# Combining a group of experts in threes behind the next group's gate/up slots

## What is computed

```python
# 4 groups x 8 experts = 32 experts, top 2 of one group for each token
def expert_block(args):
    rt, rg, e = args
    xb = x_pad[rt]
    hb = jax.nn.silu(xb @ w_gate[e]) * (xb @ w_up[e])      # 2048 -> 512
    return (hb @ w_down[e]) * rg[:, None]                  # 512 -> 2048
...
return jax.ops.segment_sum(out.reshape(P, D), row_tok, num_segments=T + 1)[:T]
```

## Time and profile before

| | |
|---|---|
| median of 3 runs | 1612.42 us (1610.18 to 1615.23) |
| span of the profiled execution | 1613.5 us |
| TensorE (PE) busy | 1272.8 us, 79% of the span |
| PE weight loads (PEld) busy | 655.1 us |
| VectorE busy | 393.7 us, 24% |
| ScalarE busy | 378.5 us, 23% |
| DMA | 475.38 MB, mean 295 GB/s over the span |
| mean granted TensorE clock | 0.896 |

### The profile page before, as it was taken

The page is one execution under the profiler, slowest core; times in us unless marked ns, Lnnn a source line. Parts: engine busy times, 40 slices in busy tenths (PEclk is TensorE's granted clock), DMA queues, the critical chain, the costliest instruction groups (busy, mean ns, idle before and its releaser), DMA issues.

```text
span 1613.5 us, 19649 instructions
## 1 busy us (share of the span) xinstructions
PE 1272.8 (79%) x7570; PEld 655.1 (41%) x7571; DVE 393.7 (24%) x737; ACT 378.5 (23%) x643; POOL 31.9 (2%) x41
## 2 busy tenths in 40 slices
PE   5999999999899996677677677568678666766765
PEld 4999998566566641221122122122122112212212
DVE  6354443245554330120120120120113012012013
ACT  5333322143433221112112112112120111211213
POOL 1001000001000000000000000000000000000000
PEclk9999999999899988888878889879897888988987
DMA  9444540123433389999989999999976998999993
GB/s 322 140 144 154 157 138 33 37 81 107 129 125 106 130 338 420 420 374 420 421 363 422 421 373 420 421 406 390 420 293 247 420 421 366 421 420 384 422 420 139
DMA packets 110801, 475.38 MB, mean 295 GB/s; under 512 B 14156, under 2 KB 51136, under 8 KB 60304
## 3 DMA queue, kind: packets, MB, share of 16 engines
q1 hardware_dynamic: 109776, 470.86, 73.3%
q0 software_dynamic: 832, 2.48, 0.4%
q10 hardware_dynamic: 64, 0.02, 0.0%
HBM read 469.96 MB, written 3.38 MB: 293 GB/s over the span
## 4 chain that ended last, share of the span: by engine, by line
PE 61%; DMA 26%; issue 7%; DVE 2%; ACT 1%; SPq 1%; ACTq 0%; DVEq 0%
DMA ring<-in_w_up 14%; PE ps L843 12%; DMA ring<-in_w_down 11%; PE ps L871 7%; PE ps L574 5%; PE ps L575 5%; PE ps L576 5%; PE ps L858 5%; PE ps L822 3%; PE ps L746 2%; PE ps L635 2%; PE ps L662 2%; PE ps L755 2%; PE ps L748 2%; PE ps L747 2%
## 5 line engine op out<-in xcount | busy, mean ns | idle before, releaser
L843 PE MATMUL ps<-ring,mix 128*32 128x512 f32 x2112 | 335.6, 772 | 242.9 <-issue 131.6
L843 PEld LDWEIGHTS ps<-ring,mix 128*32 128x32 f32 x2112 | 75.3, 131 | 495.7 <-issue 322.0
L1533 DVE TENSOR_TENSOR mix<-mix,ps 128x128 f32<-128x128 f32 x33 | 9.5, 288 | 765.5 <-ACT mix L1166 765.5
L1163 ACT COPY mix<-ps 128x512 f32<-128x512 f32 x33 | 35.5, 1076 | 616.0 <-PE ps L843 616.0
L574 PE MATMUL ps<-xT_hi,w_hi 128*128 128x320 f32 (+1 forms) x528 | 165.8, 314 | 3.9 <-DVE work L1258 3.9
L575 PE MATMUL ps<-xT_lo,w_hi 128*128 128x320 f32 (+1 forms) x528 | 164.8, 312 | 0.0
L576 PE MATMUL ps<-xT_hi,w_lo 128*128 128x320 f32 (+1 forms) x528 | 164.6, 312 | 0.0
L858 PE MATMUL ps<-ring,mix 128*32 128x512 f32 x1056 | 122.3, 596 | 29.4 <-DVE mix L1533 17.6
L871 PE MATMUL ps<-mix 128*128 128x512 f32 (+1 forms) x192 | 99.6, 678 | 23.9 <-ACT mix L1171 23.1
L822 PE MATMUL ps<-r,work 128*32 128x512 f32 (+1 forms) x816 | 107.9, 616 | 0.4 <-DVE work L1516 0.2
L1272 DVE TENSOR_TENSOR w_lo<-ring,w_hi 128x1024 fp32r<-128x1024 f32 (+1 forms) x66 | 76.8, 1205 | 117.3 <-ACT w_hi L978 117.3
(11 more groups left out here) (259 smaller groups left out, 1117.4 us busy)
## 6 DMA issues: line engine op xcount, KB each, us to landing
ring<-in_w_gate SPq DMA_DIRECT2D x128, 1024.0 KB, 20.7
ring<-in_w_up SPq DMA_DIRECT2D x128, 1024.0 KB, 22.8
ring<-in_w_down SPq DMA_DIRECT2D x128, 1024.0 KB, 23.6
ring<-in_w_in SPq DMA_DIRECT2D x32, 1024.0 KB, 8.1
ring<-in_w_o SPq DMA_DIRECT2D x16, 1024.0 KB, 6.2
hreg<-in_x_prompt SPq DMA_DIRECT2D x4, 1024.0 KB, 6.1
ring<-in_w_uq SPq DMA_DIRECT2D x4, 768.0 KB, 4.9
ring<-in_w_uv SPq DMA_DIRECT2D x2, 1024.0 KB, 5.9
```

What stands on the lines that cost most here:

```text
L843: last = pe.matmul(ps[r:r + B, 2, :], x[:, c + o, s, :], w[:, m, c + o, :], start=s == 0 and c == 0, stop=s == 3 and c == 2)
```

## The change

The 12 units of a group's combination leave the end of the iteration. They now stand in the next iteration, in threes behind `gate_up` of slots 0, 1, 2 and 3 of its first expert. Units 0 to 2 stand behind slot 0's matmuls, with the waits that stood before the whole combination. The first iteration has no group before it: it combines a `yg` and a `gT` that DVE sets to zero ahead of the loop. The last group is combined behind the loop, 12 units in a row. DVE's additions move likewise, to the head of the first expert of the next iteration. All counts of `comb_added`, `y_copied` and `gt_copied` shift by one group or one copy. Table row 2 now has the extra blocks before an expert, and a new row 4 those up to and with it.

The combination of an extra block gets a function of its own, with four banks, 4 to 7: bank `4 + n` for column block `n`. The four units of a token tile are issued together; those of the next tile wait for the addition of the same column block.

```diff
+            def combine_units(units, added_before):
+                for u in units:
                     i, n = u // 4, u % 4
                     t0, tn = TILES[i]
                     if u >= 3:
-                        pe.wait_ge(free_sem, value(u - 2))
-                    gates, rows = parts(n)
-                    pe.matmul(ps[0:tn, 5 + u % 3, :], gates[:, t0:t0 + tn], rows, ...).then_inc(full_sem, 1)
+                        pe.wait_ge(comb_added, added_before + (u - 2))
+                    pe.matmul(ps[0:tn, 5 + u % 3, :], gT[:, t0:t0 + tn], yg[:, 512 * n:512 * n + 512],
+                              start=True, stop=True).then_inc(comb_full, 1)
+
+            def combine_extra(x):
+                for i, (t0, tn) in enumerate(TILES):
+                    for n in range(4):
+                        if i:
+                            pe.wait_ge(x_added, x * 12 + (4 * (i - 1) + n + 1))
+                        rows = slice(B * n, B * (n + 1))
+                        pe.matmul(ps[0:tn, 4 + n, :], gTx[rows, t0:t0 + tn], yx[rows, :],
+                                  start=True, stop=True).then_inc(x_full, 1)
...
                     for s in range(4):
                         pe.wait_ge(slot_full[s], e * 32 + expert_count(s))
                         gate_up(xg, s).then_inc(weights_used, 1)
+                        if b == 0:
+                            if s == 0:
+                                pe.wait_ge(y_copied, q * 4 + 1)
+                                pe.wait_ge(gt_copied, q + 1)
+                                drained_extra = pe.value_load(tables[0:1, 2, bass.ds(q * 4, 1)], ...)
+                                pe.wait_ge(x_added, drained_extra)
+                                pe.wait_ge(comb_added, q * 12 + 1)
+                            combine_units(range(3 * s, 3 * s + 3), q * 12 + 1)
...
-                pe.wait_ge(y_copied, q * 4 + 4)
-                pe.wait_ge(comb_added, comb_before)
-                drained_extra = pe.value_load(tables[0:1, 2, bass.ds(q * 4 + 3, 1)], ...)
-                pe.wait_ge(x_added, drained_extra)
-                combine(lambda n: (gT, yg[:, 512 * n:512 * n + 512]), comb_full, comb_added, ...)
+            pe.wait_ge(y_copied, NE + 1)
+            pe.wait_ge(comb_added, 12 * (NE // 4) + 1)
+            drained_extra = pe.value_load(tables[0:1, 4, NE - 1:NE], ...)
+            pe.wait_ge(x_added, drained_extra)
+            combine_units(range(12), 12 * (NE // 4) + 1)
...
# VectorE
+            dve.memset(yg, 0.0).then_inc(y_copied, 1)
+            dve.memset(gT, 0.0).then_inc(gt_copied, 1)
...
                 for b in range(4):
                     e = q * 4 + b
+                    if b == 0:
+                        add_results(comb_full, lambda v: q * 12 + v, comb_added, 5, 3)
...
-                add_results(comb_full, lambda v: q * 12 + v, comb_added)
+            add_results(comb_full, lambda v: 12 * (NE // 4) + v, comb_added, 5, 3)
```

More of the change, by code:

```diff
@@ L165, in trunk_layer_kernel @@
         small = sb("small", [P, 64])
-        tables = sb("tables", [1, 4, NE], I32)
+        tables = sb("tables", [1, 5, NE], I32)
         ps = ctx.enter_context(nc.psum_tensor("ps", [P, 8, 512], F32))
@@ L468, in _ @@
                     sp.dma_start(dst, src).then_inc(slot_full[i], 16)
-            sp.wait_ge(routed, 4)
+            sp.wait_ge(routed, 5)
             with sp.Fori(1, NE) as e:
@@ L860, in down @@
                 return last
-            def combine(parts, full_sem, free_sem, value):
-                for u in range(12):
+            def combine_units(units, added_before):
+                for u in units:
                     i, n = u // 4, u % 4
@@ L868, in combine @@
                     if u >= 3:
-                        pe.wait_ge(free_sem, value(u - 2))
-                    gates, rows = parts(n)
-                    pe.matmul(ps[0:tn, 5 + u % 3, :], gates[:, t0:t0 + tn], rows, start=True, stop=True).then_inc(full_sem, 1)
+                        pe.wait_ge(comb_added, added_before + (u - 2))
[9 more added lines that the diff above has]
+                                  start=True, stop=True).then_inc(x_full, 1)
             def extra_blocks(q, comb_before, e):
@@ L879, in extra_blocks @@
                         pe.wait_ge(x_pick, x)
-                        pe.wait_ge(gt_copied, q + 1)
+                        pe.wait_ge(gt_copied, q + 2)
                         gather(pickrx, slice(0, B), x_gathered)
@@ L892, in extra_blocks @@
                         pe.wait_ge(x_hT, x)
-                        pe.wait_ge(y_copied, e + 1)
+                        pe.wait_ge(y_copied, e + 2)
                         for s in (4, 5):
@@ L899, in extra_blocks @@
                         pe.wait_ge(x_added, x * 12)
-                        combine(lambda n: (gTx[B * n:B * (n + 1), :], yx[B * n:B * (n + 1), :]), x_full, x_added, lambda v: x * 12 + v)
+                        combine_extra(x)
             for s in range(SLOTS):
@@ L910, in _ @@
             gathered_T(transposed)
-            pe.wait_ge(routed, 3)
+            pe.wait_ge(routed, 4)
             with pe.Fori(0, NE // 4) as q:
-                comb_before = q * 12 + 1
+                comb_before = q * 12 + 13
                 for b in range(4):
@@ L1193, in _ @@
             copy_xT(xg, transposed, 1, xg_ready)
-            act.wait_ge(routed, 3)
+            act.wait_ge(routed, 4)
             with act.Fori(0, NE // 4) as q:
@@ L1205, in _ @@
                         act.wait_ge(gt_full, q + 1)
-                        act.wait_ge(comb_added, q * 12 + 1)
                         act.copy(gT, ps[:, 0, 0:T]).then_inc(gt_copied, 1)
@@ L1210, in _ @@
                     extra_blocks(e)
-            used = act.value_load(tables[0:1, 2, NE - 1:NE], min_val=12, max_val=12 * 64)
+            used = act.value_load(tables[0:1, 4, NE - 1:NE], min_val=12, max_val=12 * 64)
             act.wait_ge(x_added, used)
             for i, (t0, tn) in enumerate(TILES):
-                act.wait_ge(comb_added, 12 * (NE // 4 - 1) + 4 * (i + 1) + 1)
+                act.wait_ge(comb_added, 12 * (NE // 4) + 4 * (i + 1) + 1)
                 act.activation(r2[0:tn, D * i:D * (i + 1)], xtile[0:tn, i, :], ACT.Square, accum_out=xss[0:tn, i:i + 1]).then_inc(fin_squared, 1)
@@ L1522, in pick_tokens, with add_results @@
                 dve.tensor_tensor(gpick, g[0], g[1], ALU.add).then_inc(gates_signal, 1)
-            def add_results(full_sem, value, signal):
+            def add_results(full_sem, value, signal, first_bank, banks):
                 for u in range(12):
@@ L1529, in add_results @@
                     h = xtile[0:tn, i, 512 * n:512 * n + 512]
-                    dve.tensor_tensor(h, ps[0:tn, 5 + u % 3, :], h, ALU.add).then_inc(signal, 1)
+                    dve.tensor_tensor(h, ps[0:tn, first_bank + u % banks, :], h, ALU.add).then_inc(signal, 1)
             def times_up(signal):
@@ L1556, in extra_blocks @@
                         times_up(x_hT)
-                        add_results(x_full, lambda v: before * 12 + (k * 12 + v - 12), x_added)
+                        add_results(x_full, lambda v: before * 12 + (k * 12 + v - 12), x_added, 4, 4)
             pick_tokens(link, place, P, eq, pick, pickr, gpick, pick_ready, gates_ready)
@@ L1577, in _ @@
             links = 12
-            dve.wait_ge(routed, 3)
+            dve.wait_ge(routed, 4)
             with dve.Fori(0, NE // 4) as q:
```

9 lines of the change are left out of this document (5 added, 4 removed).

## The result

| | median of runs | lowest to highest |
|---|---|---|
| kernel before | 1611.30 us (4 runs) | 1607.87 to 1615.23 |
| changed kernel | 1595.28 us (4 runs) | 1594.92 to 1595.91 |

The ratio is 0.990 with a 95% interval of 0.988 to 0.992: 13 to 19 us faster, 16 in the middle. The forecast was 1589 us, the range 1576 to 1602. A second set of runs on another chip (the first experiment) gave 1593.35 us, ratio 0.990 again.

What follows compares the result with a forecast made beforehand. Weights' transfers set the pace; time could be won only in the dips around group ends, awaiting slot 0. Savings of 25.5 + 5.1 - 7.1 = 23.5 us off 1613.5 gave 1590.0, the median 1.1 lower: 1589 us, range 1576 to 1602.

Steps and rivals of the forecast that it cites:

- the ordinary ends: Six group ends without the extra block: slot 0 freed before the combination closes the dips, 25.5 us saved.
- the pause at slot 4: Rival at ordinary group ends: 2 to 3 us of pause each remain, total 1605 to 1612 us; chance 0.15.
- due time of +44.9: Ordinary group end: slot 4 must be issued 44.9 us after the last `down` so that transfers don't pause.
- the further fetch inside the first expert: Rival: longer code adds a pause between slots 0 and 4 in eight iterations, 10 us slower, 1622 us; chance 0.05.
- nothing moves: Rival: transfers are bound by the sum of bytes, so dips come back elsewhere; chance 0.02.
- extra block: Group end with the extra block: four banks and the moved group combination save 5.1 us.
- first group: Start of the loop: 12 units on zeros delay slot 4, 7.1 us lost, between 4.0 and 10.5.
- the value taken: Ordinary group end: slot 0's issue at +17.7 us after the last `down`, in the middle of +16.8 to +18.6.
- The term of 27.4 us from slot 0 to slot 4: Issue of slot 4 after slot 0: 13.5 us as before, 12.4 for 12 units, 1.5 for the register load.
- the load's 1.5 us: Register load on TensorE's path behind slot 0: 1.5 us, half of the 3.2 us gap that held it before.
- the base of 13.5 us: Time from slot 0's issue to slot 4's in the kernel before, without units between them: 13.5 us.
- The sum by that rule: Skip and back-edge both paid in full: ordinary ends save 20.1 us, extra block 0.9 less, total 1595 us.

Runs made afterwards that it cites:

- the first experiment: The changed kernel run again unaltered, beside the kernel before on the same chip: 1593.35 us, ratio 0.990.
- the loop alone: Changed kernel with the extra block's combination in three banks as before, keeping the units in threes behind the gate/up slots: 1597.11 us, ratio 0.991.
- the turned loop: Changed kernel with the first expert ahead of the loop, iterations of experts 1, 2, 3 and the next group's 0, no combination on zeros: 1583.95 us, ratio 0.982.
- 28 increments: 28 increments of an unused semaphore at the head of TensorE's program: 1588.95 us on the kernel before, 1589.31 us on the changed kernel.
- The four banks alone: Kernel before with only the extra block's combination put on four banks: 1609.13 us, ratio 0.998.
- the eight increments: Kernel before with 8 increments of an unused semaphore at the head of TensorE's program: 1613.37 us, ratio 1.000.
- the best version: Changed kernel with the first expert ahead of the loop and units in threes, 1583.95 us; with all units behind slot 3, 1583.50 us; both ratio 0.982.

## Why the prediction was right, and where its terms were off

**The bound and the mechanism held at the ordinary ends.** The time came out of the stretches without transfers, and slot 0's issue was what ended them. Moved up to +16.2, it closed the ordinary ends: 23.5 us won against 25.5 forecast. Of the rivals, the pause at slot 4 did not come (slot 4 at +40.5 against a due time of +44.9), nor the further fetch inside the first expert, nor "nothing moves". That the sum came so near is in part luck: the three terms were off by -2.0 us (ordinary ends), -1.6 (extra block) and +2.9 (first group), and the last three rows of the table, which were in no term, add -2.0. Together that is the 2.7 us by which the span was missed.

**Slot 4 was less tight than reckoned.** It came 4.6 us early. Slot 0 itself stood 1.5 us ahead of the value taken and even below the low one (+16.2 against +17.7 and +16.8), so the skip cost nothing beyond the 3.2 us that ACT's wait had taken there. The term of 27.4 us from slot 0 to slot 4 measured 24.4: the load's 1.5 us were 0 (the units start at 590.62, slot 0's matmuls end at 590.69), and the units in threes, each behind `gate_up` of a slot, pass in 2.8 to 3.1 us (706.70, 711.61), some 11.7 us in all where 12.4 were reckoned. The rest is the base of 13.5 us, which without the units was 12.6 here, about as in the first group before (12.7). The next expert's slot 0 came 4.0 us after slot 4 (735.26 against 731.31), not 9.6.

**The first group lost less:** 4.2 us, not 7.1. Slot 4 was issued at 615.25, 2.6 us ahead of the forecast 617.8. That no pause of 4 to 5 us stands in front of the next slot 0 is a second reason, which no term had. The 4.2 us lie in the bounds that were given, 4.0 to 10.5.

**The extra block gave 3.5 us, not 5.1,** the two dips together. The combination saved 3.4 us, not 4.4. The second dip fell by 6.7, but the first rose by 3.2, and that place stood in no term: the prediction took a dip that the change doesn't touch as fixed. This is a mistake of mechanism and not of size. Its shape is seen in short stretches of the changed kernel:

```profile
1170.00:1172.00 2.00, 2.00 (x16) 0.42 (x8) 0.00 (x0) 1.02 (x1) 0.00 (x0) 0.62 0.54 221
1172.00:1174.00 2.00, 2.00 (x21) 0.75 (x14) 0.00 (x0) 0.45 (x1) 0.00 (x0) 1.00 0.46 184
1174.00:1176.00 2.00, 1.57 (x17) 1.06 (x20) 0.29 (x1) 0.99 (x3) 0.00 (x0) 1.00 0.23 94
```

The transfers don't stop, they run out over 6 us at about half, half and a quarter of the engines. In the kernel before they fall from 377 to 107 GB/s within 4 us. The end of the program loses 2.1 us in the same way (324, 197 and 209 GB/s in its last three stretches). The chain that leads to the extra block's slot 0 begins with `gate_up` of slot 3, for whose last weights TensorE waits, in the kernel before (two rows) and in the changed one:

```profile
1173.96 1.92 PE L843 MATMUL ps<-ring,mix 128*32 128x512 f32 x16 [3.04 <-DMA ring<-in_w_up]
1193.12 0.34 SPq L477 DMA_DIRECT2D ring<-in_w_gate  x1
```

```profile
1167.15 2.76 PE L843 MATMUL ps<-ring,mix 128*32 128x512 f32 x16 [3.04 <-DMA ring<-in_w_up]
```

From there to the next issue it is 19.2 us before and 19.0 after (1186.14), and 19.0 to 19.2 in every other version but the loop alone (20.1). The equal length has two reasons: before, a wait of 1.45 us for the rest of slot 5 lies on the way (1183.88), and after, TensorE has a slower stretch instead (granted clock 0.50 between 1169 and 1171). Either way the chain is as long as before. What differs is how much of slots 4 and 5, 4.2 MB, was still to be moved when it began: 3.5 MB before, 2.2 MB after. In the changed kernel nearly half of them had been moved while a piece of slot 3 was still missing, and what was left fills 5.2 us of the chain instead of 8.3: 3.1 us, the rise of the dip. The traces line up by this number: 3.4 to 3.5 MB left and a dip of 12.3 to 12.6 us in four traces, 2.8 to 3.1 MB and 13.5 to 14.1 in three, 2.0 to 2.2 MB and 15.5 to 15.8 in four (16.6 in the loop alone, with its longer chain), 1.6 MB and 17.3 in the turned loop, 1.4 MB and 19.1 in the changed kernel with 28 increments. Why the pieces get so far out of step stays open. That the sixteen engines drift apart while no pause lines them up again fits most of these (the kernel before with 28 increments has 3.5 MB left, but kept a dip of 3.7 us at the group end just before). It is argued, and no run tested it.

**The median gained less than the pair of traces.** The pair of traces differs by 20.8 us, the medians by 16.0, since the profiled execution of before was 3.9 us above the median of its four. The prediction took off 1.1 us for this. On the spans the forecast was 1590.0 against 1592.7, 2.7 us off; against the median of the four, 23.5 us less would be 1587.8, and 7.5 us were missed. Of these 7.5 us, 2.7 are the over-reckoned gain and 4.8 the difference between the pair of traces and the medians, nearly all of it the high execution of before.

**The fetch rule.** The Trainium skill, "Runtime: NRT & Kernel Launch", section "Instruction fetch mechanics", says that code is fetched in blocks of 256 instructions, ahead only in sequence, and that a taken branch out of the window waits. The sum by that rule was 1595 us, and 1595.28 was measured, but not for its reason: it had slot 0 at +18.6 and slot 4 at +46.0, and they stood at +16.2 and +40.5. What the rule does explain is the second pause, in every run that moved the code: the loop began some instructions ahead of a block's end, so that the back-edge fetched one block for 13 instructions and then waited for the next. The trace agrees: one packet of kind `instruction` in each of the two pauses, and seven packets fewer where the second pause is gone.

## What to carry to other kernels

When a pause without a releaser follows a loop's back-edge or a skipped branch, look in the view of the DMA queues for an `instruction` packet that starts in it. If a second such pause follows after a few instructions, shift the code of that engine by a few dozen harmless instructions before moving any work: here 28 of them gave 24 us, more than the change, and 8 gave nothing, so that several numbers are to be tried. Then choose what stands behind the back-edge: put there the part of the loop after which several buffers have just come free, not the one whose first buffer everything waits for. And add up dips with care: at a place where a long chain of TensorE must pass before the next transfer, what counts is how much is left to move when the chain begins, and that can shrink when earlier pauses go.

## What the runs showed of the hardware that was not expected

- A back-edge shows as one pause or as two with a few instructions between them, and which of them depends on where the code lies: 4.50 + 4.23 us in the kernel before, 4.44 + 4.41 with 8 instructions more, 4.62 alone with 28 more.
- With the transfers idle, the two pauses in front of slot 0 are 2.04 and 1.47 us in the kernel before (behind 1230.91). There the first packet of code starts between 1230 and 1231 us, about when TensorE stops; at the end at 702.33 it starts 1.7 us or more after that.
- The turned loop has a single pause of 11.96 us at its skip and back-edge, where the changed kernel has 6.93 + 3.63, and it costs no transfer.
- A register load between matmuls of different kinds did not show (590.62 against 590.69).
- The kernel before scatters more from run to run (1606.71 to 1620.50 us over 16 runs in one set) than the changed one beside it (1592.70 to 1598.52 over 5) or the turned loop (1583.01 to 1587.62 over 5). The four banks alone and the eight increments, which keep both pauses and the units ahead of slot 0, scatter as it does (16.5 and 13.7 us from lowest to highest, 11 and 10 runs). On the whole its slower executions have the lower mean clock (0.889 at 1620.50, 0.903 at 1606.71); whether that is cause or consequence stays open.
- What is left in the best version is above all the dips of the extra block, 17.3 and 5.2 us, where TensorE's chain through the block must be over before slot 0 is free (19 us up to the first issue, as above).
